# Stick-breaking attention: the two heads of a pair side by side, in rows of the array for the scores and in columns for the outputs

## What is computed

```python
def stick_breaking_attention(q, k, v):
    """A[t,s] = sigmoid(z_ts) * prod_{s<j<t} (1 - sigmoid(z_tj)), s < t only."""
    ...
        z = jnp.einsum('bhqd,bhkd->bhqk', q_blk, kh).astype(jnp.float32) * inv_sqrt
        mask = key_pos[None, :] < q_pos[:, None]
        log_1m_beta = jnp.where(mask, jax.nn.log_sigmoid(-z), 0.0)
        suffix = lax.cumsum(log_1m_beta, axis=3, reverse=True) - log_1m_beta
        a = jnp.where(mask, jnp.exp(jax.nn.log_sigmoid(z) + suffix), 0.0)
        return jnp.einsum('bhqk,bhkd->bhqd', a, vh.astype(jnp.float32)).astype(q.dtype)
    ...
        o = stick_breaking_attention(...)
        y_attn = o @ w_proj_attn[l]
        merged = jax.nn.sigmoid(ga) * y_conv + jax.nn.sigmoid(gb) * y_attn
```

## Time and profile before

| | us |
|---|---|
| median of 3 runs | 3250.92 (3246.46 to 3253.4) |
| the profiled execution | 3249.1 |
| its span in the trace | 3247.3 |
| PE busy | 3083.7 (95%) |
| DVE busy | 1671.9 (51%) |
| ACT busy | 754.3 (23%) |
| POOL busy | 1110.1 (34%) |
| mean granted TensorE clock | 0.972 |
| L1368 (outputs), PE busy, x576 | 83.9 |
| L1368, PEld busy | 75.1 |
| L2300 (scan), DVE busy, x64 | 96.5 |

### The profile page before, as it was taken

The page is one execution under the profiler, slowest core; times in us unless marked ns, Lnnn a source line. Parts: engine busy times, 40 slices in busy tenths (PEclk is TensorE's granted clock), DMA queues, the critical chain, the costliest instruction groups (busy, mean ns, idle before and its releaser), DMA issues.

```text
span 3247.3 us, 40237 instructions
## 1 busy us (share of the span) xinstructions
PE 3083.7 (95%) x14878; PEld 2494.5 (77%) x14878; DVE 1671.9 (51%) x2023; ACT 754.3 (23%) x1395; POOL 1110.1 (34%) x764
## 2 busy tenths in 40 slices
PE   7998998998989999999979999999999899999997
PEld 6885666887878888888858887766877788888886
DVE  4463444654167777777762102777232544444446
ACT  3222454222231111111140002554113211111111
POOL 3321002442753333333373332010337533333333
PEclk9997999998999999999989999997999999999999
DMA  3200000000423222323221111000223111111111
GB/s 114 58 20 13 7 4 1 1 1 20 150 79 89 78 84 79 89 78 90 71 91 50 51 42 33 14 7 1 65 88 107 39 52 50 41 52 52 51 42 62
DMA packets 211179, 171.73 MB, mean 53 GB/s; under 512 B 13367, under 2 KB 186702, under 8 KB 211086
## 3 DMA queue, kind: packets, MB, share of 16 engines
q1 hardware_dynamic: 158430, 135.34, 13.8%
q10 hardware_dynamic: 52656, 35.13, 3.6%
...
## 4 chain that ended last, share of the span: by engine, by line
PE 87%; DVE 5%; POOL 4%; ACT 2%; issue 2%; DMA 1%; SPq 0%; DVEq 0%; ACTq 0%; POOLq 0%
PE ps L865 12%; PE ps L867 12%; PE ps L866 12%; PE ps L1217 7%; PE ps L1218 7%; PE ps L1219 7%; PE ps L1035 4%; PE ps L1368 2%; PE ps L1348 2%; PE ps L1000 2%; PE ps L980 2%; PE ps L884 1%; PE ps L886 1%; PE ps L885 1%; PE ps L1188 1%
## 5 line engine op out<-in xcount | busy, mean ns | idle before, releaser
L216 POOL TENSOR_SCALAR slab_hi<-raw 128x1024 fp32r<-128x1024 f32 (+1 forms) x236 | 261.5, 1108 | 1586.5 <-PE ps L867 590.1
L219 POOL TENSOR_TENSOR slab_lo<-raw,slab_hi 128x1024 fp32r<-128x1024 f32 (+1 forms) x236 | 576.7, 2443 | 19.7
L865 PE MATMUL ps<-act_hi,slab_hi 128*128 128x512 f32 x1472 | 576.5, 392 | 3.6 <-DVE o_feat_lo L1866 1.7
L867 PE MATMUL ps<-act_hi,slab_lo 128*128 128x512 f32 x1472 | 574.2, 390 | 0.0
L866 PE MATMUL ps<-act_lo,slab_hi 128*128 128x512 f32 x1472 | 574.0, 390 | 0.0
L2215 DVE TENSOR_TENSOR acc<-ps,acc 128x512 f32<-128x512 f32 x512 | 339.4, 686 | 200.7 <-PE ps L1219 200.6
L1217 PE MATMUL ps<-slab_hi,hid_hi 128*128 128x512 f32 x1024 | 404.0, 395 | 7.2 <-DVE hid_lo L2206 3.8
L1218 PE MATMUL ps<-slab_hi,hid_lo 128*128 128x512 f32 x1024 | 400.1, 391 | 0.0
L1219 PE MATMUL ps<-slab_lo,hid_hi 128*128 128x512 f32 x1024 | 399.9, 390 | 0.0
L865 PEld LDWEIGHTS ps<-act_hi,slab_hi 128*128 128x128 f32 x1472 | 277.0, 188 | 61.5 <-DVE o_feat_lo L1866 1.9
L867 PEld LDWEIGHTS ps<-act_hi,slab_lo 128*128 128x128 f32 x1472 | 276.7, 188 | 57.9
...
## 6 DMA issues: line engine op xcount, KB each, us to landing
...
```

The lines of the kernel that those rows point to most:

```text
L216: pool.tensor_scalar(self.hi[s][:, 0:width], self.raw[r][:, 0:width], 1.0, 0.0, ALU.mult, ALU.add)\
L219: pool.tensor_tensor(self.lo[s][:, 0:width], self.raw[r][:, 0:width], self.hi[s][:, 0:width].bitcast(F32), ALU.subtract).then_inc(self.spl ...
L865: pe.matmul(o, hi[:, w], a_hi[:, k, cols], start=(k == 0), stop=False)
L867: mm = pe.matmul(o, lo[:, w], a_hi[:, k, cols], start=False, stop=(k == nk - 1))
```

## The change

Both heads of a pair now go through PE together, by tile and not by item.

- `sb_scores(i, t)` computes both heads' scores of a tile, chunk by chunk with the heads alternating, in every second step; it waits for the copies of both items before it.
- `sb_outputs(i, t)` computes both heads' outputs of a tile, four items late instead of three. Operands are exchanged: 64 columns of v are the stationary operand and the 128 columns of `sb_at` are streamed; head 0 writes partitions 0 to 63 of bank 6 and head 1 partitions 64 to 127, alternating with each block. The result is feature-major.
- `sb_at` has four buffers instead of two, and a transpose now waits for the exp that read its PSUM bank.
- The copies out of bank 6 move from DVE to ACT (`sb_out`).
- At the end the turning of `o2` is gone. ACT copies `o2` to `o2_hi` and DVE subtracts for `o2_lo`, pair by pair, and PE computes the second gate panel ahead of waiting for them (`o2_split`).
- The first pair's four projections use banks 4 to 7 instead of bank 7 alone.

The diff, cut to its core:

```diff
-SB_LAG_TURN, SB_LAG_PV = 2, 3
+SB_LAG_TURN, SB_LAG_PV = 2, 4
...
-        sb_at = [sb(f"sb_weights_t{i}", 201 + 2 * i, [P, HALF]) for i in range(2)]
-        o2 = sb("o2_tok", 57, [P, NT, CONV2])
+        sb_at = [sb(f"sb_weights_t{i}", kb, [P, HALF]) for i, kb in enumerate((201, 203, 205, 71))]
+        o2 = sb("o2_feat", 57, [P, CONV2_PANELS, SEQ])
...
-                    pe.wait_ge(sem("proj_read"), 4 * i + (4 * MLA_HEADS + n + 1))
-                o, cols = ps[:, 7, :], slice(h * HALF, (h + 1) * HALF)
+                    if i:
+                        pe.wait_ge(sem("proj_read"), 4 * i + (4 * MLA_HEADS + n + 1))
+                o, cols = ps[:, 7 if i else 4 + n, :], slice(h * HALF, (h + 1) * HALF)
...
+            def sb_scores(i, t):
+
                 n, q, kk = (t + 1) * P, q2[i % 2], k2[i % 2]
...
+                pe.wait_ge(sem("sb_z_copied"), SB_ITEMS * i + 2 * t + 2)
                 for f in range((n + HALF - 1) // HALF):
                     w = min(HALF, n - f * HALF)
-                    mm = pe.matmul(ps[:, 2 * (s % 2) + f, 0:w], q[rows, t * P:(t + 1) * P],
-                                   kk[rows, f * HALF:f * HALF + w], start=True, stop=True)
-                mm.then_inc(sem("sb_scores"), 1)
+                    for h in range(2):
+                        rows = slice(h * SB_DIM, (h + 1) * SB_DIM)
+                        mm = pe.matmul(ps[:, 2 * h + f, 0:w], q[rows, t * P:(t + 1) * P],
+                                       kk[rows, f * HALF:f * HALF + w], start=True, stop=True)
+                        if f == (n - 1) // HALF:
+                            mm.then_inc(sem("sb_scores"), 1)
...
                 for n, g in enumerate(sb_groups(s)):
+                    if SB_GROUPS * i + g >= 2:
+                        pe.wait_ge(sem("sb_at_done"), SB_GROUPS * i + g - 1)
...
+            def sb_outputs(i, t):
+
+                if t % 4 == 0:
+                    pe.wait_ge(sem("sb_o_done"), 2 * i + t // 4 + 2)
+                pe.wait_ge(sem("sb_at_done"), SB_GROUPS * i + sb_groups(2 * t + 1)[-1] + 1)
+                for b in range(t + 1):
+                    for h in range(2):
+                        at = sb_at[sb_groups(2 * t + h)[b // 4] % 4]
+                        mm = pe.matmul(ps[h * SB_DIM:(h + 1) * SB_DIM, 6, t % 4 * P:(t % 4 + 1) * P], v2[:, b, 2 * i + h, :],
+                                       at[:, b % 4 * P:(b % 4 + 1) * P], start=(b == 0), stop=(b == t))
+                mm.then_inc(sem("sb_pv"), 1)
...
-                    if s + 1 < SB_ITEMS:
-                        sb_scores(i, s + 1)
-                    if late := lagged(i, before, s, SB_LAG_PV, SB_ITEMS):
-                        sb_outputs(*late)
+                    if s % 2 and s + 1 < SB_ITEMS:
+                        sb_scores(i, s // 2 + 1)
+                    if s % 2 == 0 and s < 12 and not last:
+                        sb_project(i + 1, s // 3, SB_THIRDS[s % 3])
+                    if s % 2 == 0 and (late := lagged(i, before, s, SB_LAG_PV, SB_ITEMS)):
+                        sb_outputs(late[0], late[1] // 2)
                     if late := lagged(i, before, s, SB_LAG_TURN, SB_ITEMS):
                         sb_turn(*late)
-                    if s < 12 and not last:
+                    if s % 2 and s < 12 and not last:
                         sb_project(i + 1, s // 3, SB_THIRDS[s % 3])
...
-            for h in range(2):
-                turn("sb_o", o2, h, lambda k: pe.wait_ge(sem("sb_o_done"), SB_HEADS + 2), CONV2_PANELS)
-            turn_done("sb_o", 1, CONV2_PANELS)
             merge_gate(R9, 1, 0, 1)
+            pe.wait_ge(sem("o2_split"), CONV2_PANELS)
             merge(R9, 1, o2_hi, o2_lo)
...
+            def sb_out(i, half):
+
+                act.wait_ge(sem("sb_pv"), NT * i + 4 * half + 4)
+                act.copy(o2[:, i, half * HALF:(half + 1) * HALF], ps[:, 6, :]).then_inc(sem("sb_o_done"), 1)
...
-            for h in range(2):
-                norm_full("sb_o", h, o2_hi, nk=CONV2_PANELS)
+            for i in range(SB_PAIRS):
+                if i == SB_PAIRS - 1:
+                    sb_out(i, 1)
+                act.wait_ge(sem("sb_o_done"), 2 * i + 4)
+                act.copy(o2_hi[:, i, :], o2[:, i, :]).then_inc(sem("o2_hi_done"), 1)
+            act.wait_ge(sem("o2_split"), CONV2_PANELS)
             merge_gates(R9, 1, attn_gate)
...
-            for h in range(2):
-                norm_split("sb_o", h, o2_hi, o2_lo, nk=CONV2_PANELS)
+            dve.wait_ge(sem("sb_pv"), NT * SB_PAIRS)
+            for i in range(SB_PAIRS):
+                dve.wait_ge(sem("o2_hi_done"), i + 1)
+                dve.tensor_tensor(o2_lo[:, i, :], o2[:, i, :], o2_hi[:, i, :].bitcast(F32), ALU.subtract).then_inc(sem("o2_split"), 1)
```

58 lines of the change are left out of this document (21 added, 37 removed).

## The result

The changed kernel takes 3202.23 us (median of 4 runs, 3200.36 to 3205.76) against 3248.69 for the kernel before on the same chip: a ratio of 0.9857, 95% interval 0.984 to 0.9874. The profiled execution took 3203.56 us, its span is 3201.7. So it is 46.5 us faster; the forecast was 3198, with a range of 3188 to 3215.

The account below looks back on a forecast made before the run. PE was taken to bound the first three pairs, a DVE copy wait and low clock the last. Savings 2.5 + 10.7 + 2 x 9.6 + 19.7 = 52.1 us off 3249.1 gave 3197.0, stated as 3198, range 3188 to 3215.

Parts of the forecast that it names:

- Scores and outputs: PE in each pair: both heads overlap, so scores fall from 15.4 to 7.7 us and outputs from 16.1 to 7.7.
- Rival 1: Outputs on PE: the two column groups do not overlap; taken as 3213 us, between 3216 and 3208; chance 0.15.
- Rival 2: Scores and outputs on PE: strict program order adds one instruction per tile or run; 3207 us, chance 0.08.
- the 0.39 us for each change between full-array products and scores: PE in a middle pair: 16 places where it goes to scores and back, 0.39 us each, 6.2 us in all.
- DVE is late next: Middle pairs: DVE bounds tiles 0, 6 and 7, PE tiles 1 to 5; 57.8 us instead of 67.4.
- 0.5 for scans that run beside POOL's splits: Middle pairs, DVE: an allowance of 0.5 us in the 57.8 for scans beside POOL's splits.
- The start: First pair's projections: PE's three waits for ACT to read bank 7 go, 2.5 us less.
- The last pair and the end: Last pair, gate panel and end: DVE bounds the pair; 90.6 us falls to 70.9, 19.7 less.
- So I take it that the clock falls to half here too: Last pair, late tiles: PE's pauses halve the clock, costing 1.2 + 2.7 + 1.5 = 5.4 us, the 1.5 for the gate panel.
- rival 3: Last pair: the clock stays up, 5.4 us less, 3192; chance 0.16.
- rival 4: Middle pairs: the clock falls after pauses at tiles 7 and 0, up to 5 us in each of three pairs; 3213, chance 0.07.
- The second gate panel's cover: End of the stage: 8.1 us of copy, cast and subtractions lie hidden under the second gate panel's 10.9 us.

Follow-up runs that it names:

- cols_apart: Changed kernel, but each tile's outputs go head by head (all blocks of head 0, then all of head 1): 3213.38 us.
- rows_apart: Changed kernel, but each tile's scores go head by head (both chunks of head 0, then both of head 1): 3200.10 us.
- spread_late_split: spread_clear, with POOL's second-slab split also held until DVE has copied tiles 0 and 1 of the next pair: 3188.40 us.
- late_split: Changed kernel, with POOL's second-slab split held from tile 6 until DVE has copied tiles 0 and 1 of the next pair: 3197.22 us.
- spread_clear: Changed kernel, projections spread over steps 0 to 14, with other work between each half's end and the next half's start: 3193.99 us.
- one_bank: Changed kernel, with the first pair's four projections back in bank 7 alone: 3204.31 us.
- old_copy_on_act: Kernel before the change, with only the two copies a pair out of bank 6 moved from DVE to ACT: 3234.55 us.

## Why the forecast held, and where it was off

**Scores and outputs (right).** The forecast's 7.7 us each for scores and outputs in a pair rest on 0.107 us for two instructions. In the profile after it is 0.055 us an instruction for outputs and 1.99 us for a tile's eight scores. Rival 1, columns that don't overlap, was taken as 3213; cols_apart, which takes away most of the overlap, measured 3213.38. That the two agree so closely is luck: cols_apart keeps some overlap, and 3213 was taken between 3216 and 3208. Rival 2, strict program order, is out by rows_apart: 3200.10. PE's own work was forecast at 51.3 us a middle pair; at a clock of 1.00 throughout it is 51.31 (spread_late_split). In it, the 0.39 us for each change between full-array products and scores was what the sum left over; the row named for it shows 1.36 - 1.07 = 0.29.

**DVE is late next (right, size too small).** The tiles were forecast at 7.6 + 34.1 + 6.8 + 8.8 + 0.5. In the profile after they are 7.5, then 34.7 for tiles 1 to 5, 7.59 and 9.80. Two terms were mis-sized. "0.5 for scans that run beside POOL's splits" measured 1.6, as the split of the second slab falls on tiles 6 and 7, where DVE is the bound. And tiles 1 to 5 had no term for bank 7, where PE waits 0.8 us once a pair for ACT's read: tile 3 takes 6.96 us where 6.0 were forecast, the others some 0.1 less than forecast. Another 0.2 us lie in tiles 6 and 7, which without the split still take 15.79 where 15.6 were forecast. The clock of 0.95 in the last tile cost nothing: at 1.00, in the next pair, it takes 9.82. In the first pair (52.28 for 50.0) late_split takes 1.6 of the 2.3. spread_clear takes 4.6, more than the wait at bank 7, since it also moves projections from PE-bound to DVE-bound steps; the two do not add up, as both together take 4.8.

**The start (right).** -2.5 forecast, -3.0 measured, and one_bank gives the 3.0 back.

**The last pair and the end (direction right, a cost that didn't come).** "So I take it that the clock falls to half here too", with 5.4 us for it, is the step that failed. The waits were as forecast, up to 2.00 us in each of the late tiles, but the clock stayed up there; it was low only at the pair's start, in tile 0, around the wait of 2.46 us (0.67 from 2178 to 2185 us, a mean of 0.93 over the pair; low is 1.2 GHz, half of 2.4). The pair took 49.3 where 48 + 3.9 were forecast, the gate panel 10.88 as at full speed, the end 6.92 for 6.6. So rival 3 is what happened in this profiled execution: it was priced at -5.4, and the measured term is 3.8 below the forecast's. Of the 23.5 us, 17.9 come with the copy alone, as old_copy_on_act showed.

But whether the clock falls in the late tiles differs from one execution to the next, with the same code. one_bank has the changed kernel's last pair. Its windows of the whole pair and of part of tiles 4 and 5, and PE's scores of tile 7 (1.99 us at full clock):

```profile
2178.29:2227.94 49.65, 36.13 (x265) 23.55 (x265) 45.48 (x63) 32.41 (x59) 0.00 (x0) 0.83 0.00 1
2199.00:2206.00 7.00, 6.42 (x31) 3.89 (x29) 6.62 (x10) 4.00 (x8) 0.00 (x0) 0.52 0.01 2
...
2219.01 3.11 PE L1355 MATMUL ps<-k_feat,q_feat 64*128 64x512 f32 x8 [1.88 <-DVE sb_z L2318]
```

Here the clock did fall, as the forecast said, and the pair took 49.65 us all the same, 0.6 more than the changed kernel's 49.05: each fall lasted for a part of a tile, and PE's pauses took most of it in. In late_split the pair has a mean clock of 0.87 and takes 49.8, and the gate panel behind it 12.7 at 0.87, so that there the forecast's 1.5 for a slow panel did come. So the price was wrong more than the fall: in these two runs it cost 0.6 and 2.3 us, not 5.4.

**The clock in the middle pairs (rival 4, its mechanism came, its price didn't).** It did fall after the pauses of 2.4 us at the pairs' turns, means of 0.96 and 0.98, where the forecast had 1. But it fell in tile 0 and the last us of tile 7, where PE has slack; of "up to 5 us in each of three pairs" nothing can be seen in the changed kernel. In late_split and spread_clear the same fall met tile 1 and cost 1.6 us, and in one_bank, whose pairs have the changed kernel's code, a longer one made the third pair 60.3 us.

**The second gate panel's cover (right, size too large).** "0.2 + 5.9 + 2.0 = 8.1 us" took the subtraction from a row in which it lasts 1.97 us; here it takes 1.22, and the last of the four ended 4.8 us behind the last output. Nothing of it was on the path.

**The sum.** Of the 52.1 us forecast, 5.9 did not come in the first three pairs, and 4.3 more came in the start and at the end: 50.5. That the sum is off by 1.6 only is partly luck, as the two errors cancel. The profiled execution's 3203.56 lies 6.6 us above the 3197.0 forecast for it: the 1.6, 4.8 ahead of the stage, where nothing was changed, and 0.1 behind it. How the median's 4 us above 3198 divide can't be said, as one execution alone has a profile. The profiled executions of the other kernels differ there as well (the first of the 96 products begins at 1978.3 us in rows_apart, at 1981.9 in old_copy_on_act); what makes that scatter was not tried.
